# The gated scan: keys as logarithms inside the exponents, wider query products, an earlier exponential

## What is computed

```python
def _hgrn2_gate(z, lb):
    f = lb + (1.0 - lb) * jax.nn.sigmoid(z)
    logf = jnp.log(jnp.maximum(f, F_TINY))
    k = (1.0 - lb) * jax.nn.sigmoid(-z)
    return logf, k

def step(state, inp):                        # one chunk of 64 tokens
    qt, kt, vt, bt = inp                     # bt: running sum of logf
    diff = bt[:, :, :, None, :] - bt[:, :, None, :, :]
    decay = jnp.where(lower, jnp.exp(jnp.where(lower, diff, 0.0)), 0.0)
    scores = jnp.einsum('bhtk,bhsk,bhtsk->bhts', qt, kt, decay)
    o = (jnp.einsum('bhts,bhsv->bhtv', scores, vt)
         + jnp.einsum('bhtk,bhkv->bhtv', qt * jnp.exp(bt), state))
    b_last = bt[:, :, -1:, :]
    state = (jnp.exp(b_last[:, :, 0, :])[..., None] * state
             + jnp.einsum('bhsk,bhsv->bhkv', kt * jnp.exp(b_last - bt), vt))
    return state, o
```

## Time and profile before

| | us |
|---|---|
| median of 3 runs | 3474.61 (3471.65 to 3475.27) |
| profiled execution, span and own time | 3475.4 |
| scan of layer 2, first to last instruction of VectorE | 2040.0 to 2202.5 |
| one pass of the input projection on TensorE | 12.09 |

### The profile page before, as it was taken

How to read it: one execution, slowest core, us unless ns; L and a number is a source line. 1 busy time by engine, 2 the same in 40 slices (tenths; PEclk the granted TensorE clock), 3 DMA queues, 4 the chain that set the end, 5 groups by cost and what they waited for, 6 DMA issues and landing times.

```text
span 3475.4 us, 44870 instructions
## 1 busy us (share of the span) xinstructions
PE 3315.4 (95%) x16138; PEld 2538.4 (73%) x16138; DVE 2112.2 (61%) x3509; ACT 969.1 (28%) x2203; POOL 1588.7 (46%) x1534
## 2 busy tenths in 40 slices
PE   8989999999999999999999988999999987899998
PEld 5665555555557967888888756688888865678887
DVE  7577756544544296555646668478764776656554
ACT  2076211001021174211122264222213244332211
POOL 1054322222235224444454467456645547655654
PEclk9999999999999999999999989999999998999999
DMA  7300223333312201345432200244443200022222
GB/s 254 130 10 7 97 98 120 104 122 114 107 58 73 79 2 37 122 158 170 158 96 85 64 12 11 85 156 158 153 143 99 86 28 18 12 88 88 88 89 79
DMA packets 91129, 317.87 MB, mean 91 GB/s; under 512 B 10816, under 2 KB 13152, under 8 KB 90912
## 3 DMA queue, kind: packets, MB, share of 16 engines
q1 hardware_dynamic: 64224, 218.34, 19.5%
q10 hardware_dynamic: 24768, 90.19, 7.1%
q0 software_dynamic: 1920, 6.49, 0.7%
HBM read 312.88 MB, written 2.10 MB: 91 GB/s over the span
## 4 chain that ended last, share of the span: by engine, by line
PE 86%; DVE 7%; ACT 3%; POOL 2%; issue 2%; DMA 0%; DVEq 0%; ACTq 0%; SPq 0%; POOLq 0%
PE ps L1336 66%; PE ps L1338 4%; PE ps L631 3%; PE ps L1293 2%; PE ps L1006 1%; PE ps L1246 1%; PE ps L992 1%; PE ps L1028 1%; PE ps L1189 1%; DVE arena L2626 1%; PE ps L1231 1%; PE ps L1064 1%; ACT arena L1520 1%; DVE arena L2584 1%; PE ps L1261 1%
## 5 line engine op out<-in xcount | busy, mean ns | idle before, releaser
L1336 PE MATMUL ps<-arena 128*128 128x256 f32 (+1 forms) x3744 | 952.4, 408 | 0.2
L1336 PEld LDWEIGHTS ps<-arena 128*128 128x128 f32 x3744 | 710.8, 190 | 204.9 <-issue 1.7
L2757 POOL TENSOR_TENSOR arena<-ring,arena 128x512 f32<-128x512 f32 (+1 forms) x140 | 182.6, 1304 | 836.8 <-PE ps L1336 836.8
L1336 PE MATMUL ps<-arena,ring 128*128 128x256 f32 (+1 forms) x2032 | 524.9, 410 | 3.1 <-ACT arena L1690 3.1
L1336 PE MATMUL ps<-hbuf,ring 128*128 128x256 f32 (+1 forms) x1824 | 469.4, 407 | 4.2 <-ACT hbuf L1797 1.2
L1336 PEld LDWEIGHTS ps<-arena,ring 128*128 128x128 f32 x2032 | 385.3, 190 | 119.5 <-ACT arena L1690 5.9
L1336 PEld LDWEIGHTS ps<-hbuf,ring 128*128 128x128 f32 x1824 | 345.8, 192 | 113.7 <-ACT hbuf L1797 19.5
L2300 DVE TENSOR_TENSOR arena<-ps,arena 128x256 f32<-128x256 f32 (+1 forms) x192 | 86.1, 449 | 356.7 <-PE ps L1336 235.6
L2187 DVE CUSTOM_DVE_ANT_0 aring<-aring,csil,adab 128x1024 f32<-128x1024 f32 x176 | 261.7, 1508 | 1.8
L2305 DVE SCALAR_TENSOR_TENSOR resid<-ps,mod,resid 128x256 f32<-128x256 f32 (+2 forms) x296 | 137.4, 482 | 185.2 <-PE ps L1336 180.5
L2740 POOL TENSOR_TENSOR arena<-ring 128x512 f32<-128x512 f32 (+1 forms) x140 | 182.1, 1301 | 141.2 <-PE ps L1336 133.6
(11 more groups left out here) (324 smaller groups left out, 5342.3 us busy)
## 6 DMA issues: line engine op xcount, KB each, us to landing
aring<-in_ada ACTq DMA_DIRECT2D x172, 512.0 KB, 4.7
ring<-in_mlp SPq DMA_DIRECT2D x128, 512.0 KB, 3.7
ring<-in_up SPq DMA_DIRECT2D x88, 512.0 KB, 3.3
ring<-in_in SPq DMA_DIRECT2D x56, 512.0 KB, 3.3
ring<-in_down SPq DMA_DIRECT2D x32, 512.0 KB, 3.6
ring<-in_odd_in SPq DMA_DIRECT2D x24, 512.0 KB, 3.3
arena<-in_ada SPq DMA_DIRECT2D x16, 512.0 KB, 13.7
ring<-in_out SPq DMA_DIRECT2D x16, 512.0 KB, 3.3
```

Of the source, the lines that this page charges most:

```text
L1336: return nc.tensor.matmul(ps[:, bank, 0:p.tw], w, x, start=start, stop=stop, skip_group_check=True)
L2757: nc.gpsimd.tensor_tensor(s[3], f0[:, h:2 * h], s[1], ALU.subtract).then_inc(wsum_ready, 1)
```

## The change

The scan needs key times decay in many places. Before, decays were exponentials and keys were multiplied in afterwards. Now the logarithm of the key is added to the exponent ahead of the exponential. The keys are clamped from below and split in two factors like the gates, in `clamps` (two more instructions for each block, and one that is now waited for; six blocks per layer); ScalarE takes two more logarithms per block in `logarithm`; GpSimd adds them; and VectorE builds six key sums per layer in the attention stage (`sum_keys`), logarithm of the key plus or minus E. `weigh_levels` and the key half of `weigh_ends` go. The queries are laid out so that two instructions of 64x256 make a level instead of four of 64x128. In ScalarE's scan, `level_decays(u + 1)` moves ahead of `keep_early` and `take_levels`.

```diff
+KEY_TINY = 2.0 ** -120
...
-            return (X, H)[k // 4][:, 2 * (k % 4):2 * (k % 4) + 2, S:T]
+            j = k % 4
+            return (X, H)[k // 4][:, 4 * (j // 2):4 * (j // 2) + 4, S + P * (j % 2):S + P * (j % 2) + P]
...
+        def log_key(r):
+            return tail_block(H, r) if r < 4 else LK45[:, r - 4, :].rearrange("p (a t) -> p a t", a=2)
+        def log_key_low(r):
+            return tail_block(X, r) if r < 4 else PB2[:, r - 3, :].rearrange("p (a t) -> p a t", a=2)
...
                             if li == 0:
-                                pe.wait_ge(level_weighed, 2 * blk + d + 1)
+                                pe.wait_ge(level_decay, 2 * blk + d + 1)
...
                     act.wait_ge(gate_clamped, 6 * mixer_phases.index(i) + b + 1)
+                    nc.scalar.activation(log_key(b), log_key(b), ACT.Ln)
+                    nc.scalar.activation(log_key_low(b), log_key_low(b), ACT.Ln)
                     nc.scalar.activation(LF[:, b, :], LF[:, b, :], ACT.Ln)
...
                     take_pairs(u)
+                    level_decays(u + 1)
                     keep_early(EARLY_AT.get((u, "levels"), ()))
                     take_levels(u)
-                    level_decays(u + 1)
...
                         cumulate(range(2 * (p - 1), 2 * p) if 1 <= p <= 12 else ())
+                        if p >= 3 and p % 2:
+                            sum_keys(layer - 2, (p - 3) // 2)
...
+                nc.vector.tensor_tensor(key_sum(r).rearrange("p (a c k) -> p a c k", a=2, c=2), log_key(r).rearrange("p a (c k) -> p a c k", c=2), e,
+                                        ALU.add if d else ALU.subtract).then_inc(keys_summed, 1)
...
-                nc.vector.tensor_scalar(KR[:, b, :], KR[:, b, :], OMLB[:, b:b + 1], None, ALU.mult)
+                chain(nc.vector.tensor_scalar(KR[:, b, :], KR[:, b, :], OMLB[:, b:b + 1], KEY_TINY, ALU.mult, ALU.max))
+                key = KR[:, b, :].rearrange("p (a t) -> p a t", a=2)
+                nc.vector.tensor_scalar(log_key_low(b), key, SPLIT, 1.0, ALU.mult, ALU.min)
+                nc.vector.tensor_scalar(log_key(b), key, 1.0 / SPLIT, None, ALU.max)
...
-                        nc.vector.tensor_tensor(w[:, :, 0], bd, x[:, :, 0], ALU.subtract)
-                        nc.vector.tensor_tensor(w[:, :, 1], x[:, :, 1], bd, ALU.subtract)
+                        if d == 0:
+                            nc.vector.tensor_tensor(w[:, :, 0], bd, k[:, :, 0], ALU.add)
+                            nc.vector.tensor_tensor(w[:, :, 1], x[:, :, 1], bd, ALU.subtract)
...
-                    nc.vector.tensor_tensor(KF[:, d, :], KF[:, d, :], KR[:, 3 * d + b, :], ALU.mult)
...
-                def weigh_levels(u):
...
-                        x = nc.vector.tensor_tensor(w, w, k, ALU.mult)
-                    x.then_inc(level_weighed, 1)
...
-                    weigh_levels(u + 1)
...
                             nc.gpsimd.tensor_tensor(LF[:, b, :], LF[:, b, :], LTMP[:, b, :], ALU.add)
+                            nc.gpsimd.tensor_tensor(log_key(b), log_key(b), log_key_low(b), ALU.add)
...
-                                for half in range(2):
-                                    x = nc.gpsimd.tensor_tensor(dst[rows, half, hx], w[rows, 2 * half:2 * half + 2],
-                                                                q[rows, 2 * half:2 * half + 2], ALU.mult)
+                                x = nc.gpsimd.tensor_tensor(dst[rows, hx], w[rows], q[rows], ALU.mult)
```

More of the change, by code:

```diff
@@ L441, in build, with tail_block, key_sum @@
         ONE1 = carve(P)
+        LK45 = carve(2 * S, "p (b t) -> p b t", b=2)
+        AR_TAIL = aring[:, :, :].rearrange("p s d -> p (s d)")[:, 6 * 4 * 129:6 * 4 * 129 + S]
+        def tail_block(half, j):
+            return half[:, 2 * j:2 * j + 2, S:T]
+        def log_key(r):
+            return tail_block(H, r) if r < 4 else LK45[:, r - 4, :].rearrange("p (a t) -> p a t", a=2)
+        def log_key_low(r):
+            return tail_block(X, r) if r < 4 else PB2[:, r - 3, :].rearrange("p (a t) -> p a t", a=2)
+        def key_sum(r):
+            return (csil[:, 1, 0:S], csil[:, 1, S:2 * S], JUNK[:, 0:S], AR_TAIL, LK45[:, 0, :], LK45[:, 1, :])[r]
         consts_in = sem("consts_in")
@@ L513, in build @@
         level_decay = sem("level_decay")
-        level_weighed = sem("level_weighed")
+        keys_summed = sem("keys_summed")
         query_ready = sem("query_ready")
@@ L1246, in scan @@
                                 mm = nc.tensor.matmul(ps[:, 2 + v % 2, t * P:(t + 1) * P], WL[:, 7 * (1 - d) + li, t * P:(t + 1) * P],
-                                                      level_queries(v)[:, t // 2, t % 2 * P:(t % 2 + 1) * P], start=True, stop=True)
+                                                      level_queries(v)[:, t, :], start=True, stop=True)
                             mm.then_inc(level_ready, 1)
@@ L1840, in end_decays @@
                     src = e[:, :, 1 - d:129 - d]
-                    plain, ends = ((QF, KF), (KF, QF))[d]
+                    keys = key_sum(3 * d + b).rearrange("p (t k) -> p t k", t=4)
                     act.wait_ge(cumulated, 6 * n + u + 1)
-                    nc.scalar.activation(plain[:, d, :].rearrange("p (t k) -> p t k", t=4), src, ACT.Exp)
+                    act.wait_ge(keys_summed, 6 * n + u + 1)
+                    plain, of = ((QF, src), (KF, keys))[d]
+                    nc.scalar.activation(plain[:, d, :].rearrange("p (t k) -> p t k", t=4), of, ACT.Exp)
                     for t in range(4):
-                        nc.scalar.activation(ends[:, d, t * P:(t + 1) * P], src[:, t, :], ACT.Exp, scale=-1.0, bias=e[:, t, 128:129])
+                        if d == 0:
+                            nc.scalar.activation(KF[:, d, t * P:(t + 1) * P], keys[:, t, :], ACT.Exp, bias=e[:, t, 128:129])
+                        else:
+                            nc.scalar.activation(QF[:, d, t * P:(t + 1) * P], src[:, t, :], ACT.Exp, scale=-1.0, bias=e[:, t, 128:129])
                     nc.scalar.activation(ET[:, 3 * d:3 * d + 2], e[:, 1:3, 128], ACT.Exp)
@@ L2169, in cumulate, with sum_keys @@
                         x.then_inc(cumulated, 1)
+            def sum_keys(n, u):
+                d, r = u % 2, 3 * (u % 2) + u // 2
+                if u >= 6:
+                    return
+                dve.wait_ge(cumulated, 6 * n + u + 1)
+                e = E[:, r, :, 1 - d:129 - d].rearrange("p (a c) k -> p a c k", a=2)
+                nc.vector.tensor_tensor(key_sum(r).rearrange("p (a c k) -> p a c k", a=2, c=2), log_key(r).rearrange("p a (c k) -> p a c k", c=2), e,
+                                        ALU.add if d else ALU.subtract).then_inc(keys_summed, 1)
             def modulate(share):
@@ L2574, in level_exponents @@
                     dve.wait_ge(cumulated, 6 * n + u + 1)
+                    dve.wait_ge(keys_summed, 6 * n + u + 1)
+                    keys = key_sum(3 * d + b).rearrange("p (t k) -> p t k", t=4)
                     if u == 1:
@@ L2645, in scan @@
                 weigh_ends(0)
-                weigh_levels(0)
                 for u in range(6):
```

14 lines of the change are left out of this document (6 added, 8 removed).

## The result

The changed kernel takes 3488.9 us, median of 5 runs (3486.7 to 3494.8), against 3475.2 (3471.7 to 3482.1) for the kernel before, timed on the same chip. The ratio is 1.0038, with a 95% interval of 1.0028 to 1.0049: slower by 13 us (10 to 17). The forecast was 3488.

What follows compares the result with a forecast made beforehand. TensorE (95% busy) bounds the in-projection; in scan and attention the chain goes between engines. The terms, 2 x (8 + 4) + 2 x 1.5 - 14 = +13 us, gave 3488 us, range 3467 to 3505.

Steps and rivals of the forecast that it cites:

- VectorE's part of the projection: In-projection: added `clamps` instructions meet GpSimd's sums and delay TensorE; 8 us per layer, bounds 1.8 and 9.2.
- one-by-one turns: In-projection: `clamps` instructions and GpSimd's sums alternate singly; VectorE's round 15.2 us, TensorE's waits 9.2 per layer.
- the middle bound: In-projection: the three unchained `clamps` instructions go through together; VectorE's round 13.9 us, costing 5.3 per layer.
- rival 3: In-projection: new TensorE stalls lower its clock, 1.7 us a pass in ten passes; 3505 us; 0.13 together with Rival 4.
- GpSimd's part: In-projection: two more additions ahead of S2 make TensorE wait in three passes; 4.0 us per layer, 2.8 to 5.2.
- The key sums: Attention stage: six sums of about 0.65 us on VectorE, mostly in gaps; 1.5 us per layer, bounds 0.5 and 2.5.
- The scan: Layers 2 and 3: without `weigh_levels` each scan wins 6.9 us, between 0 and 9; both win 14.
- the first unit: Scan: exponents and queries start earlier, though the moved exponential delays plain levels; 4.5 to 5.9 us won, 5.2 taken.
- units 1 and 3: Scan: the exponential now in series takes back most of `weigh_levels`' 4.4 us each; 1.7 us won together.
- Rival 1: In-projection: VectorE keeps the path and stalls stay small, clamps cost 1.8 us per layer; 3473 us; chance 0.19.
- Rival 2: Scan: its waits also lowered TensorE's clock, so removing them gains more; 3461 us; chance 0.13.
- Rival 4: Scan: queries meet the exponents throughout, so the scan returns nothing; 3502 us; chance 0.13 together with rival 3.

Runs made afterwards that it cites:

- both_back: The changed kernel with the queries back as four instructions of 64x128 and ScalarE's exponential back behind `take_levels`: 3474.1 us, ratio 0.9996.
- exponential_back: The changed kernel with only ScalarE's exponential (`level_decays`) moved back behind `take_levels`: 3487.5 us, ratio 1.0028 to the kernel before.
- dummy_weighing: The changed kernel with seven unused multiplications of 128x256 and their wait put back where `weigh_levels` stood: 3516.1 us, ratio 1.0119.
- taps_last: The changed kernel with the convolution's taps behind the two `clamps` calls in passes 4 to 6: 3486.2 us, ratio 1.0033.

## Why the forecast held, point by point

**VectorE's part of the projection, forecast 8 per layer.** Held, and by the mechanism named: instructions of `clamps` that meet a sum of GpSimd wait it out one by one (four rows of 1.38 to 1.54 us), not two or three at once and not with VectorE keeping the path. The round is 14.55 us (1880.76 to 1895.31) where one-by-one turns gave 15.2 and the middle bound 13.9. The waits are two of 2.20 us where the count had three of 3.0 and 3.1; that the size came out near all the same is in part the slow matmuls (1.8 us), which the forecast had only in rival 3. Without the key additions layer 2's projection is 6.6 us longer than before, and layer 3's 9.9. Of this 9.9, 7.5 are waits (2.20 + 2.21 + 3.08) and 1.8 are slow matmuls. The Trainium skill's exclusive lock ("SBUF — State Buffer", section "Who interferes with whom") agrees with the rows of `clamps`. Of instructions with two operands in SBUF, such as taps and exponents, that section says only that they contend with GpSimd's reads; here a tap loses 0.45 us and an exponent 0.3 (beside 64x128) or 0.5 to 0.65 (beside 64x256), less than a whole GpSimd instruction; beside one addition of 128x512 an exponent lost 1.1 (1.49 us at 2054.75 in the changed kernel).

**GpSimd's part, forecast 4.0.** It measured 5.5 in layer 2, a little over the upper bound of 5.2: the waits were 1.98 + 1.58 + 1.22 = 4.8, against 2.8 without meetings. In layer 3 two such waits are left, 1.60 and 1.23 us. Both parts together were forecast at 12 and measured 12.1 and 10.5.

**The key sums, forecast 1.5.** The stages are 2.0 and 1.7 us longer, inside the bounds of 0.5 and 2.5, but the instruction was undersized. One sum takes 1.00 to 1.11 us instead of my 0.65. Each stands behind an inverse that releases a scaling on GpSimd, and all six meet one: two scalings take 1.36 to 1.68 us in the kernel before, and 2.10 beside two of the sums (at 2020.21 and 2036.02 in the changed kernel). My working had one such meeting, not six. Over all profiles, 20 stages with the sums average 59.8 us (58.3 to 61.1) and 8 without them 57.1 (55.2 to 59.0). That would be 2.8 per layer, but the two groups overlap, and no run takes out the sums alone.

**The scan, forecast -6.9.** The net is right, -7.2 and -7.7, and so are its parts by unit, nearly: the first unit gained 6.5 and 5.8 (layers 2 and 3) against 5.2, units 1 and 3 together 0.3 and 1.3 against 1.7, and the even units and the last 0.3 and 0.2 against nothing. both_back tells what lies inside them. In the first unit two errors cancelled. I had charged the moved exponential 3.2 us there; it costs nothing (32.6 and 33.3 us with it, 32.3 and 33.4 without). So my working gave `weigh_levels` 5.2 + 3.2 = 8.4 in that unit, and it is worth 6.8 and 5.7. That the first unit came out near 5.2 is luck. In units 1 and 3 the mechanism held: taking out `weigh_levels` is worth its own time, 4.0 to 5.2 us in each against 4.4, and the exponential in series takes most of it back. There the sizes are a little off: with the wide queries it takes back 10.1 and 7.4 us in the two units together, where 8.8 - 1.7 = 7.1 was the working. Over a whole scan `weigh_levels` (with the key half of `weigh_ends`) is worth 15.5 and 16.4 us, both_back against before, where my terms add up to 17.2; the two other edits give back 8.3 and 8.7, where they add up to 10.3. The change as a whole thus spends half of what its main idea wins.

**The rivals.** Rival 1 (VectorE keeps the path) fell with the rows of `clamps`. Rival 2 (a shorter scan that also raises the clock) is wrong as a time but not as a mechanism: the clock in the changed kernel's scans is 0.91 and 0.90 against 0.87 and 0.88 before, and TensorE is busy for 5.8 and 1.1 us less; how much of the 7 us that is, no run tells apart. In both_back it goes further: unit 1 runs at 1.00 instead of 0.92. Rival 3 (the clock falls behind the new stalls) happened in part, behind one wait per projection and worth 1.8 us (2.67 + 2.94 - 3.78 in layer 2, 3.66 - 1.89 in layer 3), near the 1.7 it gave a pass, but not in ten passes. Rival 4 (the queries meet the exponents throughout) happened in unit 1 for nine of fourteen exponents.

**What stays open.** Why the clock fell during the early matmuls of unit 1 in exponential_back (0.63) and not in both_back (1.00) isn't told apart: the waits ahead of them are nearly the same (0.51 and 0.58 against 0.48 us). Why the moved exponential costs nothing in the first unit was not tried either. That wide queries cost 9 us in the kernel before and nothing in the changed one is explained in part, by the multiplications that they no longer meet and by VectorE's wait of 4.5 to 6.0 us ahead of the merges; what makes up for the other 2 us isn't.

## What to carry to other kernels

A cost that was added where two engines contend is often a matter of place: look for passes in which both have slack and move the same instructions there before judging the idea. When two edits sit on parallel chains that join (here exponents on VectorE and copies on ScalarE ahead of the merges), test them together as well as alone, since either alone only uncovers the other. And an instruction that waits costs its queue the wait too, not only its own duration (the 7.25 us ahead of 4.04 in dummy_weighing's first unit); a net forecast that comes out right says nothing of its terms until they are run apart.

## What the runs showed of the chip

A short wait can cost more than itself, by an amount that hardly varies. Seven of the kernels above, the changed one among them, have TensorE waits of 2.0 to 3.1 us for VectorE in both projections, two or three in each. In all 14 projections the granted clock falls from 2.4 to 1.2 GHz behind one of these waits (in layer 3 of dummy_weighing behind two), and the matmuls take 1.5 to 1.8 us more each time. Behind which wait it falls is not in the wait's length: eight matmuls took 2.00 us after a wait of 3.00, and 3.66 after one of 2.03, where 1.89 is usual. In taps_last, where the waits for VectorE are 0.8 to 1.0 us, the clock stays full in these passes, behind a wait of 2.11 us for S2 too.

How VectorE and GpSimd share their path depends on who runs. The early output's addition of 128x512 (1.27 us alone) took 4.09 us in the changed kernel from 2062.82 on, while the exponents beside it kept their 0.41. A query of 64x256 beside the same exponents made them 0.94 to 1.06, one of 64x128 made them 0.73, and the addition of 128x512 at 2054.46 made one 1.49. So here now the one engine gives way and now the other; what decides it isn't shown.
